# Two-layer hybrid trunk: DeltaNet block inversion over eleven units, first layer's mixer steps in other slots

## What is computed

```
layer 0: h = rmsnorm(x);  proj = h @ w_in                      # 7176 columns
         mLSTM heads (4): S = (q k^T) * exp(log_d - m);  num = S v;  y = num / max(|den|, exp(-m))
                          y = sigmoid(o) * head_rmsnorm(y) * norm
         retention heads (4): rotary(q, positions), rotary(k, positions), decay mask, scores @ v
         x += concat(mLSTM, retention) @ w_out;  x += swiglu(rmsnorm(x))
layer 1: gated DeltaNet: causal conv (4 taps) and silu on q, k, v; 32 value heads
         a = strictly lower part of (k_beta k^T) * decay;  (I + a) is inverted by blocks
         o = head_rmsnorm(o) * norm * silu(z);  x += o @ w_out;  x += swiglu(rmsnorm(x))
output:  rmsnorm(x)
```

## Time and profile before

| | |
|---|---|
| median of 3 runs | 2826.89 us (2826.2 to 2827.94) |
| the profiled execution | 2829.2 us, span 2827.4 us |
| TensorE busy | 2784.0 us, 98% of the span |
| VectorE busy | 1573.5 us, 56% |
| ScalarE busy | 1373.8 us, 49% |
| GpSimd busy | 75.4 us, 3% |
| mean granted TensorE clock | 0.996 |
| DMA | 502.63 MB, mean 178 GB/s |

### The profile page before, as it was taken

One profiled execution on the slowest core, in us unless ns is written; L12 is line 12 of the kernel. 1 busy time (PEld: TensorE's weight loads), 2 busy tenths in 40 slices (PEclk: granted clock), 3 DMA queues, 4 the chain that ended last, 5 costly groups with the idle time before them and its releaser, 6 DMA issues.

```text
span 2827.4 us, 37259 instructions
## 1 busy us (share of the span) xinstructions
PE 2784.0 (98%) x13652; PEld 2303.3 (81%) x13652; DVE 1573.5 (56%) x1946; ACT 1373.8 (49%) x1877; POOL 75.4 (3%) x54
## 2 busy tenths in 40 slices
PE   9999999999999999999999999999999999999998
PEld 7788788888888888877878787887888888888886
DVE  4554565545444444557686868665555454454444
ACT  5444555444444444456565767554454444444443
POOL 0000000000000000000010101000000000000000
PEclk9999999999999999999999999999999999999999
DMA  8464466666666666655353535555666666666664
GB/s 253 143 199 149 134 193 186 193 186 188 190 188 191 186 191 188 183 168 150 120 169 122 169 123 173 168 180 179 187 189 190 188 190 189 189 189 188 205 192 149
DMA packets 261554, 502.63 MB, mean 178 GB/s; under 512 B 20144, under 2 KB 20400, under 8 KB 261168
## 3 DMA queue, kind: packets, MB, share of 16 engines
q1 hardware_dynamic: 259792, 494.60, 58.2%
q10 hardware_dynamic: 816, 3.15, 0.3%
q0 software_dynamic: 816, 3.15, 0.3%
HBM read 495.59 MB, written 5.24 MB: 177 GB/s over the span
## 4 chain that ended last, share of the span: by engine, by line
PE 92%; DVE 5%; ACT 1%; issue 1%; DVEq 1%; DMA 0%; ACTq 0%; SPq 0%
PE acc L552 28%; PE acc L546 28%; PE acc L547 28%; PE aux L599 2%; PE aux L778 2%; DVE wlo L1441 2%; DVE arena L1863 1%; DVE arena L1860 1%; PE aux L784 1%; PE aux L772 1%; PE aux L758 0%; PE aux L751 0%; DVEq L1862 0%; ACT arena L1295 0%; DVEq L1829 0%
## 5 line engine op out<-in xcount | busy, mean ns | idle before, releaser
L1441 DVE TENSOR_TENSOR wlo<-wraw,whi 128x1024 fp32r<-128x1024 f32 x928 | 1152.1, 1250 | 1024.7 <-ACT whi L988 1017.0
L988 ACT ACTIVATE whi<-wraw 128x1024 fp32r<-128x1024 f32 x928 | 977.4, 1059 | 1151.2 <-PE acc L552 1073.8
L546 PE MATMUL acc<-whi,hT_hi 128*128 128x512 f32 x2624 | 1042.2, 397 | 0.9 <-ACT arena L998 0.5
L547 PE MATMUL acc<-whi,hT_lo 128*128 128x512 f32 x2624 | 1025.8, 391 | 0.0
L552 PE MATMUL acc<-wlo,hT_hi 128*128 128x512 f32 x2624 | 707.8, 392 | 14.7 <-DVE wlo L1441 14.3
L552 PEld LDWEIGHTS acc<-wlo,hT_hi 128*128 128x128 f32 x2624 | 493.6, 189 | 124.4 <-DVE wlo L1441 21.7
L546 PEld LDWEIGHTS acc<-whi,hT_hi 128*128 128x128 f32 x2624 | 494.8, 189 | 104.3 <-issue 1.7
L547 PEld LDWEIGHTS acc<-whi,hT_lo 128*128 128x128 f32 x2624 | 495.1, 189 | 101.7 <-issue 1.7
L546 PE MATMUL acc<-whi,arena 128*128 128x512 f32 x1088 | 427.4, 393 | 3.2 <-ACT whi L988 3.2
L547 PE MATMUL acc<-whi,arena 128*128 128x512 f32 x1088 | 425.1, 391 | 0.0
L552 PE MATMUL acc<-wlo,arena 128*128 128x512 f32 x1088 | 293.4, 392 | 0.0
(11 more groups left out here) (248 smaller groups left out, 1182.7 us busy)
## 6 DMA issues: line engine op xcount, KB each, us to landing
wraw<-in_l_w_in SPq DMA_DIRECT2D x304, 512.0 KB, 4.2
wraw<-in_l_w_gate SPq DMA_DIRECT2D x176, 512.0 KB, 3.7
wraw<-in_l_w_up SPq DMA_DIRECT2D x176, 512.0 KB, 3.6
wraw<-in_l_w_down SPq DMA_DIRECT2D x176, 512.0 KB, 4.2
wraw<-in_l_w_out SPq DMA_DIRECT2D x96, 512.0 KB, 4.6
o_rounds<-arena POOLq DMA_DIRECT2D x3, 1024.0 KB, 4.7
arena<-o_rounds ACTq DMA_DIRECT2D x3, 1024.0 KB, 6.1
x<-in_x SPq DMA_DIRECT2D x4, 512.0 KB, 7.0
```

The lines of the kernel that those rows point to most:

```text
L546: nc.tensor.matmul(pair[m], hi[:, k, tok], wh, start=first, stop=False)
L547: nc.tensor.matmul(pair[m], lo[:, k, tok], wh, start=False, stop=False)
L988: nc.scalar.activation(whi[:, s, :], wraw[:, s, :], ACT.Copy).then_inc(hi_done, 1)
L1441: V.tensor_tensor(wlo[:, s, :], wraw[:, s, :], whi[:, s, :].bitcast(F32), ALU.subtract).then_inc(lo_done, 1)
```

## The change

- Angles: VectorE works them out behind unit 17 of the program, and ScalarE takes the sine behind unit 25; before, both stood in slot 0 (behind unit 34). The rotation stays in slot 0.
- mLSTM heads: three slots of TensorE a head. The sums of the next head are issued right behind the value products of a head; `rows` and the division have other places on VectorE, and the products of q and k come two units behind the sums.
- ScalarE's mixer steps stand one unit later than VectorE's, up to slot 69 (`L0_ACT_SLOTS`).
- The sigmoid stands one step ahead of the last head's squares. The gated norm of the mLSTM heads is done and signalled in two halves. The second group's transposes stand a unit earlier (slot 74 for 75).
- Rounds: the leaf's 31 steps are spread over eleven units by `LEAF_CUTS` (3, 3, 3, 2, 3, 3, 2, 3, 3, 3, 3), and all steps of `s` = 21 to 30 stand one unit later, up to `s` = 31. The step `s` = 32 and those after it stay.
- The squares of the first 128 tokens of a round's output are taken at `s` = 36 rather than 38.

```diff
-MLSTM_HEAD = ["rows", "d_psum", "d_max", "d_exp", "s_psum", "s_prod", "st_psum", "st_copy", "num_psum", "num_div"]
+MLSTM_HEAD = ["d_psum", "d_max", "d_exp", "s_psum", "s_prod", "st_psum", "st_copy", "num_psum", "num_div"]
...
+L0_ACT_SLOTS = [w if w == 0 or w > 69 else w + 1 for w in L0_SLOTS]
...
+LEAF_CUTS = (0, 3, 6, 9, 11, 14, 17, 19, 22, 25, 28, LEAF - 1)
...
                     projected(10)
                     weighted_values(st_sb, VM + h * MDV).then_inc(l0_step, 1)
+                    if h < MH - 1:
+                        decay_sums(h + 1)
...
-                if s == 30:
+                if s == 31:
                     pe.wait_ge(conv_sum, TOK_AT(r, V1))
                     token_major(V1, aux[0])
...
-                    yield
+                yield
+                nc.scalar.activation(pr[:, :, OM:OM + 1024], pr[:, :, OM:OM + 1024], ACT.Sigmoid)
                 yield
                 l0(f"m{MH - 1}_num_div")
                 head_squares(VM, MH - 1, 16)
-                head_rms(16)
-                done(nc.scalar.activation(pr[:, :, OM:OM + 1024], pr[:, :, OM:OM + 1024], ACT.Sigmoid))
+                done(head_rms(16))
...
+            def hook_a1(i, b, j):
+                hook_a(i, b, j)
+                if b == 1 and j == 1:
+                    next(mixer)
+            body("l0a", 1, 2, hook_a1)
...
-                head_norm(VM, OM, mnorm[:])
+                done(head_norm(VM, OM, mnorm[:], range(0, 2)))
+                head_norm(VM, OM, mnorm[:], range(2, 4)).then_inc(m_norm_late, 1)
...
-            body("l0a", 1, 2, nothing)
             mixer = l0_mixer()
+            body("l0a", 1, 2, lambda i, b, j: next(mixer) if b == 0 and j == 1 else None)
...
-                if 10 <= s <= 19:
-                    leaf(3 * (s - 10), 3 * (s - 10) + 3 if s < 19 else LEAF - 1)
-                if s == 19:
+                if 10 <= s <= 20:
+                    leaf(LEAF_CUTS[s - 10], LEAF_CUTS[s - 9])
+                if s == 20:
                     leaf_end()
-                if s == 21:
+                if s == 22:
                     conv(Q)
```

More of the change, by code:

```diff
@@ L121 @@
             + [f"r{h}_{s}" for h in range(RH) for s in ("s_psum", "s_dec", "o_psum", "o_copy")]
-            + [f"m{h}_{s}" for h in range(MH) for s in MLSTM_HEAD]
+            + ["m0_d_psum"]
+            + [t for h in range(MH) for s in MLSTM_HEAD[1:]
+               for t in ([f"m{h}_{s}", f"m{h + 1}_d_psum"] if s == "num_psum" and h < MH - 1 else [f"m{h}_{s}"])]
             + ["m_sq", "m_norm"]
@@ L368, in build, with l0_slots @@
         NORM_OF = {"out0": 1, "dn0": 2, "out1": 3, "dn1": 4}
-        def l0_slots(mixer, w):
-            if w in L0_SLOTS:
+        def l0_slots(mixer, w, slots=L0_SLOTS):
+            if w in slots:
                 next(mixer)
@@ L693, in l0_mixer, with decay_sums @@
                     weighted_values(rs_sb, VR + h * RD).then_inc(l0_step, 1)
-                for h in range(MH):
-                    yield
-                    l0(f"m{h}_rows")
+                def decay_sums(h):
+                    pe.wait_ge(m_rows, h + 1)
                     rows = d_rows[:, :, :].rearrange("p a b -> p (a b)")
@@ L703, in l0_mixer @@
                                      ).then_inc(l0_step, 1)
+                yield
+                l0(f"r{RH - 1}_o_copy")
+                decay_sums(0)
+                for h in range(MH):
                     yield
@@ L1244, in squares, with output_squares @@
                     act.drain()
+                def output_squares(c):
+                    for h in range(HV):
+                        a = nc.scalar.activation(flat(k_tok[:])[:, head(h)], o_r[:, c, head(h)], ACT.Square,
+                                                 accum_out=small(6, HV * c + h, 1))
+                    return a
                 def exps(c):
@@ L1347, in gdn @@
                     nc.scalar.activation(o_r[:, 1, :], aux[0][:, :], ACT.Copy).then_inc(end_act, 1)
+                    act.wait_ge(end_dve, END_DVE(r, "o0"))
+                    output_squares(0)
+                    act.drain()
                 if s == 38:
                     act.wait_ge(end_dve, END_DVE(r, "o1"))
-                    for c in range(M):
-                        for h in range(HV):
-                            a = nc.scalar.activation(flat(k_tok[:])[:, head(h)], o_r[:, c, head(h)], ACT.Square,
-                                                     accum_out=small(6, HV * c + h, 1))
-                        act.drain()
-                    a.then_inc(o_sq, 1)
+                    output_squares(1).then_inc(o_sq, 1)
+                    act.drain()
                 if s == 41:
@@ L1617, in head_norm @@
                     dve.drain()
-                    a = V.tensor_tensor(pr[:, :, base:base + 1024], pr[:, :, base:base + 1024],
-                                        pr[:, :, gate_col:gate_col + 1024], ALU.mult)
-                done(a)
+                    first, last = heads[0] * 256, heads[-1] * 256 + 256
+                    a = V.tensor_tensor(pr[:, :, base + first:base + last], pr[:, :, base + first:base + last],
+                                        pr[:, :, gate_col + first:gate_col + last], ALU.mult)
+                return a
             def rows(h):
@@ L1712, in l0_mixer, with divided @@
                     yield
+                def divided(h):
+                    for m in range(M):
+                        a = V.tensor_scalar(pr[:, m, VM + h * MDV:VM + (h + 1) * MDV], aux4[2][:, m * 256:(m + 1) * 256],
+                                            col(6, 6 + m, 7 + m), None, ALU.mult)
+                    done(a)
+                rows(0)
                 for h in range(MH):
-                    l0("r3_o_copy" if h == 0 else f"m{h - 1}_num_div")
-                    rows(h)
                     yield
                     l0(f"m{h}_d_psum")
+                    if h:
+                        divided(h - 1)
                     V.tensor_tensor(d_sb[:], aux4[0][:, 0:3 * P], C["neg"], ALU.add)
@@ L1735, in l0_mixer @@
                     done(V.reciprocal(col(6, 6, 8), col(6, 4, 6)))
+                    if h < MH - 1:
+                        rows(h + 1)
                     yield
-                    yield
-                    l0(f"m{h}_num_psum")
-                    for m in range(M):
-                        a = V.tensor_scalar(pr[:, m, VM + h * MDV:VM + (h + 1) * MDV], aux4[2][:, m * 256:(m + 1) * 256],
-                                            col(6, 6 + m, 7 + m), None, ALU.mult)
-                    done(a)
+                yield
+                l0(f"m{MH - 1}_num_psum")
+                divided(MH - 1)
                 yield
                 l0("m_sq")
-                head_norm(VM, OM, mnorm[:])
+                done(head_norm(VM, OM, mnorm[:], range(0, 2)))
+                head_norm(VM, OM, mnorm[:], range(2, 4)).then_inc(m_norm_late, 1)
                 for g in range(4):
@@ L1755, in l0_mixer @@
                         dve.wait_ge(acc_read[1], BLOCK0["out0"] // 2)
-                        head_norm(VR, GR, None, range(2, 4))
+                        done(head_norm(VR, GR, None, range(2, 4)))
                     yield
```

55 lines of the change are left out of this document (30 added, 25 removed).

## The result

| | median us | runs | lowest to highest |
|---|---|---|---|
| before | 2826.55 | 4 | 2825.67 to 2827.94 |
| changed | 2811.51 | 4 | 2811.18 to 2812.04 |

The changed kernel takes 0.9946 of the time of the kernel before (95% interval 0.9934 to 0.9958), which is 15.0 us less; the prediction said 18.3 less (2808.3). Its profiled execution took 2811.72 us with a span of 2809.9, 17.5 us less than the span before.

What follows compares the result with a forecast made beforehand. TensorE, busy 2784.0 of 2827.4 us, was taken to bound the kernel. The terms 4.4 + 2.1 + 2.5 + 6.0 + 3.6 = 18.6 us, off the median of 2826.89, gave 2808.3 us, range 2804.1 to 2815.5.

Steps and rivals of the forecast that it cites:

- Angles: First mixer, TensorE's wait at 121 us: moving the angles away removes it and its clock loss, 4.4 us (2.7 to 4.7).
- Heads: mLSTM heads: TensorE's three waits for the exponentials go, as a unit more stands ahead of the products, 2.1 us (0 to 2.6).
- end of the mixer: Gated norms ending the first mixer: earlier sigmoid and halved norm remove TensorE's waits, 2.5 us (1.5 to 2.5).
- Rival 2: Mixer: the new order makes TensorE wait at another step, half of 2.1 + 2.5 lost, 2810.6 to 2812.9; chance 0.13.
- Rounds, stall: Leaf's end in four rounds: one more unit leaves VectorE 1.5 us less late each, 6.0 us (4.8 to 6.5).
- edits at nothing: Rounds: shifted steps, GpSimd's shorter distance and squares at `s` = 36, each cost 0, at most 0.5 us a round.
- Rounds, clock: Leaf's end in three rounds: shorter stalls no longer bring TensorE's clock down, 3.6 us (0 to 6.7).
- Rival 1: TensorE's clock still falls behind shorter stalls; 1.7 + 3.6 = 5.3 us are missing, 2813.6; chance 0.15.
- rival 4: At `s` = 32 TensorE waits for the scaled values in each round; slower, over 2832.5; chance 0.02.
- rival 3: Behind `conv(Q)` VectorE isn't less late, so the 6.0 and 3.6 us stay where they are, 2817.9; chance 0.05.

Runs made afterwards that it cites:

- first trace: The kernel before, unchanged, in the profiled execution that the prediction was read from: 2829.2 us.
- second trace: The kernel before, unchanged, profiled once more after the change was measured: 2826.71 us for the profiled execution, 2826.32 in the median of eight.

## Why the prediction was right, and where it was off

- **Angles, 4.4.** Right: 4.7 us in the first trace, of which 1.7 are clock. Against the second trace, without that fall, 3.2; alone on the chip 3.1. The range (2.7 to 4.7) had named this end.
- **Heads, 2.1, and end of the mixer, 2.5.** The waits went as worked out, 2.1 and 2.5 us. The terms were too small: 3.4 and 3.0 were measured, above their own ranges (up to 2.6 and 2.5). For three slots fewer I counted 0. The heads gained 1.3 us beyond the waits, 0.4 for each slot, so each change from a unit to another kind of work and back may cost about that. This is read off the two traces and no run tests it.
- **The step that failed** is a sentence in the heads: "ScalarE's steps stand a unit later; it used to sit waiting there, so this costs nothing as long as it is ahead." I looked at the heads only. `L0_ACT_SLOTS` also moves the gates' step, where ScalarE's waiting was the cover itself: it had loaded its table before VectorE came. This cost 4.0 us. Rival 2 named the mechanism (ScalarE a unit later makes TensorE wait at another step) and had neither the place nor the size (2.3).
- **Rounds, stall, 6.0.** Right in size in the third round: it gained 1.5 us, as forecast, with no fall in either trace. The split is another than I had it. I took all 1.5 off TensorE's wait, and the wait at the leaf's end fell by 0.9; the other 0.6 are shorter distances between matmuls, which the prediction doesn't have and no run explains. Against the second trace the second round can be read without the clock too, and it gained 1.9. One wait of 0.9 to 1.6 us stays at each leaf's end and 0.6 behind the convolution, as said; the fourth round has one of 0.6 more, ahead. That this stall is VectorE's backlog was shown by moving its start. The extra 1.1 us are the squares, which I had put among the edits at nothing.
- **Rounds, clock, 3.6.** Right in kind: no falls in the rounds at stalls up to 1.6 us, here and in each kernel that has them. Rival 1 is refuted there. The size hung on one execution: against the second trace the rounds gain 10.0 us in all and not 11.9. The share of one half that I took from comparing two rounds was rough: the second round with its fall and without it differs by 0.7 us between the two traces of before, where I had 0.9. In the first round, with 6.8 us at the lower level, more came back than the 1.8 I counted: it gained 4.2 us for 3.3 forecast.
- **Rest.** No wait at step 32 (rival 4), and the convolution's wait is no longer than it was (rival 3). The fall at `out1` is none of the change's doing: eleven of thirteen traces have it, and the first trace of before was one of the two without.
- **The sum.** Against the first trace: heads and end 1.8 too small, squares 1.1, rounds 1.2, angles 0.3 and the start 0.2; the new wait 4.0 and the fall at `out1` 1.6 not foreseen. To a tenth this is 17.5 in place of 18.6. The other 2.5 us up to the 15.0 measured come from the base. I took gains read from a profiled execution of 2829.2 us off a median of 2826.9. That execution spent 17.1 us at the lower level while TensorE worked, and the second trace 13.7; it also began its units 0.8 us later. Both were among the gains. Against the second trace of before, 2826.7 us, the changed kernel gains 15.0. Of the 3.2 us between forecast and result most is this base and the new wait, less what the small terms gave back. That it came so close is in part luck: 5.6 us not foreseen stand against 4.6 us of terms that were too small.

## What to carry to other kernels

When one number moves a whole table of steps, walk it step by step: an engine that sits waiting at a step may be the cover of another, with its table load done before the value comes. In a queue that runs in order, the copies that the bound engine needs, itself or by way of another engine, go ahead of an instruction that waits for that same engine; two such turns gave 7.1 and 5.7 us here. And a gain of clock read from one trace is one draw: take it as a chance times a price, and don't subtract it from the median of other runs.

## What was new about the hardware

- Whether TensorE's clock falls is not decided by the wait's length alone, but falls get more frequent with it: none of 96 up to 1.81 us, 14 of 23 from 2.0 to 2.3, 11 of 13 at 3.15, all four over 4.2 and these twice as long (6.8 us for 3.4). The same wait of the same kernel had a fall in one execution and none in the next. So to shorten a wait from 2.2 to 1.5 us gains more than the 0.7 on average.
- A wait of 2 us costs up to 1.8 us more in clock, as behind the gates (4.0 in all); at the leaf's end, where another wait for VectorE follows, 0.7 to 0.8 us of it reached the end.
- Behind a table load of 1.28 us the tanh began 0.02 us later (157.94 + 1.28, and 159.24), and the same holds behind each of the changed kernel's other table loads but two, which wait for TensorE. So the load is the whole price of the switch here.
